# Narrow contractions unpadded, paired indexer units and earlier releases in a hybrid attention, mLSTM and MoE block

## The reference

```python
idx_score = einsum('bqh,bqhs->bqs', wib, relu(einsum('bqhd,bsd->bqhs', qib, ki)))   # 8 heads, d = 32
_, sel = lax.top_k(idx_score, 256)
logits = einsum('bqgrd,bqkgd->bqgrk', qb, ks) * scale                               # 8 heads, 2 key heads, d = 64
p = softmax(where(valid, logits, -inf)); out = einsum('bqgrk,bqkgd->bqgrd', p, vs)
```

```python
gu = xb @ w_gu[e] + b_gu[e]                   # 1024 x 2048 weights of each expert
act = glu * sigmoid(1.702 * glu) * (lin + 1)
y = act @ w_dn[e] + b_dn[e]                   # 1024 x 1024
```

## Time and profile before

| | us |
|---|---|
| median of three runs (2430.87 to 2431.50) | 2431.18 |
| the profiled execution | 2432.87 |
| its span, first to last instruction | 2431.1 |
| PE busy | 2223.4 (91%) |
| PE weight loads busy | 1799.6 (74%) |
| DVE busy | 1814.3 (75%) |
| ACT busy | 1374.4 (57%) |
| POOL busy | 527.8 (22%) |

### The profile page before, as it was taken

The page is one execution under the profiler, slowest core; times in us unless marked ns, Lnnn a source line. Parts: engine busy times, 40 slices in busy tenths (PEclk is TensorE's granted clock), DMA queues, the critical chain, the costliest instruction groups (busy, mean ns, idle before and its releaser), DMA issues.

```text
span 2431.1 us, 41797 instructions
## 1 busy us (share of the span) xinstructions
PE 2223.4 (91%) x15519; PEld 1799.6 (74%) x15519; DVE 1814.3 (75%) x2070; ACT 1374.4 (57%) x1547; POOL 527.8 (22%) x458
## 2 busy tenths in 40 slices
PE   6879999859979769999999999999999999999994
PEld 5667888748967557777777777777778778777773
DVE  3679999935442478778778778778877877877885
ACT  4451223756652346666666666666666657667664
POOL 1006786770020011111111111111101102102120
PEclk9989999869989879999999999999999999999997
DMA  5011211020012258798898898888989889889897
GB/s 142 13 35 35 53 51 45 31 83 1 1 51 104 101 211 311 278 332 299 295 332 289 304 323 306 308 316 301 315 303 318 316 294 325 315 281 333 314 323 273
DMA packets 253534, 526.47 MB, mean 217 GB/s; under 512 B 32984, under 2 KB 59736, under 8 KB 253116
## 3 DMA queue, kind: packets, MB, share of 16 engines
q1 hardware_dynamic: 240204, 483.27, 55.6%
q0 software_dynamic: 13264, 42.34, 6.7%
HBM read 490.96 MB, written 35.91 MB: 217 GB/s over the span
## 4 chain that ended last, share of the span: by engine, by line
PE 66%; DMA 10%; DVE 6%; ACT 5%; issue 5%; SPq 5%; POOL 4%; ACTq 0%; DVEq 0%; POOLq 0%
PE ps L1749 12%; PE ps L1751 11%; PE ps L1750 11%; DMA e_raw<-in_w_gate_up_dram 9%; PE ps L1428 6%; PE ps L1430 6%; PE ps L1429 6%; PE ps L1756 5%; PE ps L1629 2%; SPq L726 2%; PE ps L1619 1%; PE ps L1761 1%; DVE e_wlo L2256 1%; ACT e_whi L1311 1%; SPq L728 1%
## 5 line engine op out<-in xcount | busy, mean ns | idle before, releaser
L2256 DVE TENSOR_TENSOR e_wlo<-e_raw,e_whi 128x2048 fp32r<-128x2048 f32 x410 | 927.2, 2286 | 120.9 <-ACT e_whi L1311 118.1
L1311 ACT ACTIVATE e_whi<-e_raw 128x2048 fp32r<-128x2048 f32 x411 | 784.0, 1916 | 377.2 <-PE ps L1751 200.1
L1749 PE MATMUL ps<-e_whi,xh 128*128 128x512 f32 x1088 | 436.0, 401 | 6.4 <-DVE e_wlo L2256 6.2
L1750 PE MATMUL ps<-e_whi,xl 128*128 128x512 f32 x1088 | 424.5, 390 | 0.0
L1751 PE MATMUL ps<-e_wlo,xh 128*128 128x512 f32 x1088 | 424.2, 390 | 0.0
L937 POOL DMA_INDIRECT x_d<-ym,scur x34 | 71.8, 2110 | 926.2 <-ACT ym L1344 905.6
L1749 PEld LDWEIGHTS ps<-e_whi,xh 128*128 128x128 f32 x1088 | 204.2, 188 | 64.9 <-issue 23.9
L1749 PE MATMUL ps<-e_whi,ath 128*128 128x512 f32 x544 | 222.4, 409 | 22.3 <-DVE atl L2284 20.8
L1751 PEld LDWEIGHTS ps<-e_wlo,xh 128*128 128x128 f32 x1088 | 204.3, 188 | 44.1
L1750 PEld LDWEIGHTS ps<-e_whi,xl 128*128 128x128 f32 x1088 | 204.4, 188 | 38.8
L1751 PE MATMUL ps<-e_wlo,ath 128*128 128x512 f32 x544 | 214.0, 393 | 0.0
(11 more groups left out here) (358 smaller groups left out, 3562.5 us busy)
## 6 DMA issues: line engine op xcount, KB each, us to landing
e_raw<-in_w_gate_up_dram SPq DMA_DIRECT2D x275, 1024.0 KB, 6.3
e_raw<-in_w_down_dram SPq DMA_DIRECT2D x136, 1024.0 KB, 7.8
w_raw<-in_w_in_dram SPq DMA_DIRECT2D x20, 512.0 KB, 3.8
xt<-in_x_dram SPq DMA_DIRECT2D x8, 512.0 KB, 6.2
wo_raw<-in_w_out_dram SPq DMA_DIRECT2D x8, 512.0 KB, 6.7
xr<-in_x_dram SPq DMA_DIRECT2D x8, 512.0 KB, 4.3
x_d<-x SPq DMA_DIRECT2D x8, 512.0 KB, 2.6
h_d<-h SPq DMA_DIRECT2D x8, 512.0 KB, 2.9
```

The source lines that it names most:

```text
L1311: nc.scalar.activation(e_whi[:, m % HRING, :], e_raw[:, m % RING, :], ACT.Copy).then_inc(s.e_hi, 1)
L1749: nc.tensor.matmul(dst, a_hi, slot_hi, start=False, stop=False, skip_group_check=True)
L1750: nc.tensor.matmul(dst, a_lo, slot_hi, start=False, stop=False, skip_group_check=True)
L2256: nc.vector.tensor_tensor(e_wlo[:, m % HRING, :], e_raw[:, m % RING, :], e_whi[:, m % HRING, :].bitcast(F32), ALU.subtract).then_inc(s.e_l ...
```

## The change

1. **Indexer.** `iq_hi` and `iq_lo` keep the queries as they come, 128 rows by two groups of 128 columns. A head is a block of 32 rows of it, and the matmul takes these rows of queries and of keys alone. One copy on ACT and one subtraction on DVE make a query tile. PE issues two units at a time, each of the three terms for the one and then for the other, on different rows of the array. The units have four homes in PSUM (`unit_out`) in place of two. The five gate steps on ACT follow units 3, 6, 9, 12 and 15. POOL's zeroing of `iq_hi` and `iq_lo` is gone, and so is the wait for it.
2. **Attention.** `q_hi` and `q_lo` are kept the same way, four groups of 128 columns; a head is 64 rows. POOL's zeroing is gone. ACT's `k_hi` and first `q_hi` stand ahead of turn c = 8 of the mLSTM loop, and PE's `scores(0)` and `scores(1)` in turn c = 9, ahead of the last transposes of `m_hn`. PE's order is transposes(u), scores(u + 2), values(u - 1). The buffers that move for this put `wo_raw` elsewhere.
3. **Experts.** A piece whose slot was last used by an "S" or an "X" unit is loaded when DVE has made its low part (`e_lo`), no longer when PE has finished it. For slots last used by an "L" unit nothing changes.

```diff
-        iq_hi = at("iq_hi", Q0, [P, 2, IH, P], F32R)
+        iq_hi = at("iq_hi", Q0, [P, 2, 2, P], F32R)
...
-        q_hi = at("q_hi", M0, [P, 2, HEADS, P], F32R)
+        q_hi = at("q_hi", X0, [P, 2, 4, P], F32R)
...
+        def unit_out(u):
+
+            return ps[:, u % 4, :] if u < 2 * IH else pair(2 * ((u + 2) % 4))
...
             def load(u, m, e):
 
-                sp.wait_ge(s.p_pc, u.nth(PIECES, m + 1))
+                before = u.kind if m >= RING else {"L": "S", "S": "L", "X": "X"}[u.kind]
+                if before == "L":
+                    sp.wait_ge(s.p_pc, u.nth(PIECES, m + 1))
+                else:
+                    sp.wait_ge(s.e_lo, u.nth(PIECES, m + 1))
...
-                if f == 1:
-                    gp.wait_ge(s.p_ht, NT)
-                    nc.gpsimd.memset(iq_hi[:].bitcast(F32), 0.0)
-                    nc.gpsimd.memset(iq_lo[:].bitcast(F32), 0.0).then_inc(s.g_zero, 1)
...
-            gp.wait_ge(s.p_in, NT)
-            nc.gpsimd.memset(q_hi[:].bitcast(F32), 0.0)
-            nc.gpsimd.memset(q_lo[:].bitcast(F32), 0.0).then_inc(s.g_zero, 1)
...
-                        for g in range(4):
-                            rows = slice(ID * g, ID * g + ID)
-                            nc.scalar.activation(iq_hi[rows, i % 2, g::4, :], iqt[rows, :, i * P:(i + 1) * P], ACT.Copy).then_inc(s.a_iqhi, 1)
+                        nc.scalar.activation(iq_hi[:, i % 2, :, :], iqt[:, :, i * P:(i + 1) * P], ACT.Copy).then_inc(s.a_iqhi, 1)
...
-                        if u >= 22 and (u - 22) % 4 == 0 and (u - 22) // 4 < 5:
-                            gate_step((u - 22) // 4)
+                        if u in (3, 6, 9, 12, 15):
+                            gate_step(u // 3 - 1)
...
+                if c == NT:
+                    act.wait_ge(s.g_rq, 15)
+                    act.wait_ge(st_mo[0], 32)
+                    act.wait_ge(st_mo[1], 32)
+                    nc.scalar.activation(k_hi[:], kt[:], ACT.Copy).then_inc(s.a_qkhi, 1)
+                    q_hi_of(0)
...
-                if f == 5:
-                    pe.wait_ge(s.a_gate, 2)
+                if f in (4, 5):
+                    pe.wait_ge(s.a_relu, 6 * IH - 7 + f)
...
-            for u in range(6 * IH):
+            for u in range(0, 6 * IH, 2):
...
-                if u >= 2:
-                    pe.wait_ge(s.a_relu, u - 1)
+                if u == 2 * IH:
+                    pe.wait_ge(s.a_iwt, 1)
+                    pe.wait_ge(s.a_gate, 2)
+                elif u >= 4:
+                    pe.wait_ge(s.a_relu, u - 2)
...
-                    m = product(pair(2 * (u % 2))[:, a:b], iq_hi[:, i % 2, h, :], iq_lo[:, i % 2, h, :], ik_hi[:, a:b], ik_lo[:, a:b],
-                                True, True)
-                m.then_inc(s.p_is, 1)
+                    for n, (q_, k_) in enumerate(((iq_hi, ik_hi), (iq_hi, ik_lo), (iq_lo, ik_hi))):
+                        for e in range(2):
+                            rows = slice(ID * ((h + e) % 4), ID * ((h + e) % 4) + ID)
+                            m = nc.tensor.matmul(unit_out(u + e)[:, a:b], q_[rows, i % 2, (h + e) // 4, :], k_[rows, a:b],
+                                                 start=(n == 0), stop=(n == 2))
...
+                rows = slice(HD * (h // 4), HD * (h // 4) + HD)
+                    m = product(pair(2 * (u % 2))[:, a:b], q_hi[rows, i % 2, h % 4, :], q_lo[rows, i % 2, h % 4, :],
+                                k_hi[rows, a:b], k_lo[rows, a:b], True, True)
...
+                if c == NT + 1:
+                    pe.wait_ge(s.a_nd, NT)
+                    scores(0)
+                    scores(1)
...
                     transposes(u)
+                if u + 2 < NT * HEADS:
+                    scores(u + 2)
                 if u >= 1:
                     values(u - 1)
-                if u + 2 < NT * HEADS:
-                    scores(u + 2)
```

More of the change, by code:

```diff
@@ L706, in load, with loads @@
                     sp.dma_start(dn_piece(e_raw, slot), src).then_inc(s.ld_g[slot], 16)
-            def loads(u, here, following):
+            def loads(u, here, after, following):
                 for m in range(3, PIECES):
@@ L733, in _ @@
                 en = sp.value_load(be_d[bass.ds(j + ROW_X + 1, 1), 0:1], min_val=0, max_val=E - 1)
-                loads(Unit(j, 1, 2 * LARGE, "X"), ex, en)
+                loads(Unit(j, 1, 2 * LARGE, "X"), ex, "X", en)
             last = Unit(nl, 1, 2 * LARGE, "X")
             sp.wait_ge(s.st_yo, 16 * LARGE + 16)
-            for done, value in ((s.e_lo, last.nth(PIECES, 2)), (s.e_hi, last.nth(PIECES, 3)),
+            for done, value in ((s.e_lo, last.nth(PIECES, RING + 2)), (s.e_hi, last.nth(PIECES, 3)),
                                 (s.p_pc, last.nth(PIECES, RING)), (s.st_y, last.nth(16, 16))):
@@ L1224, in _ @@
             act.wait_ge(s.g_mix, NT)
-            act.wait_ge(s.g_rq, 15)
-            nc.scalar.activation(k_hi[:], kt[:], ACT.Copy).then_inc(s.a_qkhi, 1)
-            def q_hi_of(i):
-                if i == 0:
-                    act.wait_ge(s.g_zero, 4)
-                if i >= 2:
-                    act.wait_ge(s.p_s, HEADS * (i - 1))
-                for g in range(KVH):
-                    rows = slice(HD * g, HD * g + HD)
-                    nc.scalar.activation(q_hi[rows, i % 2, 4 * g:4 * g + 4, :], qt[rows, :, i * P:(i + 1) * P], ACT.Copy).then_inc(s.a_qkhi, 1)
-            q_hi_of(0)
             exp(0)
@@ L1598, in _ @@
                     m_weights(c + 1)
-            def scores(u):
-                i, h = u // HEADS, u % HEADS
-                w = P * (i + 1)
-                if u >= 2:
-                    pe.wait_ge(s.v_msk, u - 1)
-                if h == 0:
-                    pe.wait_ge(s.v_qklo, 2 * (i + 1) + 1)
-                for a in range(0, w, 512):
-                    b = min(a + 512, w)
-                    m = product(pair(2 * (u % 2))[:, a:b], q_hi[:, i % 2, h, :], q_lo[:, i % 2, h, :], k_hi[:, a:b], k_lo[:, a:b],
-                                True, True)
-                m.then_inc(s.p_s, 1)
             def transposes(u):
@@ L2011, in q_lo_of @@
             def q_lo_of(i):
-                for g in range(KVH):
-                    rows = slice(HD * g, HD * g + HD)
-                    dve.wait_ge(s.a_qkhi, 2 * i + g + 2)
-                    nc.vector.tensor_tensor(q_lo[rows, i % 2, 4 * g:4 * g + 4, :], qt[rows, :, i * P:(i + 1) * P],
-                                            q_hi[rows, i % 2, 4 * g:4 * g + 4, :].bitcast(F32), ALU.subtract).then_inc(s.v_qklo, 1)
+                dve.wait_ge(s.a_qkhi, i + 2)
+                nc.vector.tensor_tensor(q_lo[:, i % 2, :, :], qt[:, :, i * P:(i + 1) * P],
+                                        q_hi[:, i % 2, :, :].bitcast(F32), ALU.subtract).then_inc(s.v_qklo, 1)
             q_lo_of(0)
@@ L2201, in _ @@
             assert d.n == DEST_STEPS, d.n
+            dve.sem_inc(s.e_lo, RING)
+            dve.wait_ge(s.e_lo, RING)
             hot = Steps(dve, s.v_hot)
```

62 lines of the change are left out of this document (36 added, 26 removed).

## The result

The changed kernel is slower, by about 1%. Its median of ten executions is 2462.2 us (2440.43 to 2488.21), against 2431.42 us (2430.87 to 2433.78) for ten of the kernel before on the same chip, 31 us more. The ratio, which leaves the longest three executions out, is 1.0112 with a 95% interval of 1.0089 to 1.0135. The prediction was 2407.6 us. The ten times stand in three groups, near 2440, 2462 and 2487 us, with a mean granted clock of PE (the profile gives it as a share of full speed) of 0.932, about 0.921 and 0.910 to 0.915. The kernel before spreads over 3 us.

What follows compares the result with a forecast made beforehand. PE was taken to set the pace in most stages, DVE in the indexer, a short chain ahead of attention. Terms -14.5 - 7.1 + 14 - 16 = -23.6 us from the median of 2431.18 gave about 2407.6 us, range 2387 to 2424.

Steps and rivals of the forecast that it cites:

- the clock in attention: Attention: case of PE's clock staying low there, counted among the slower outcomes; chance 0.06.
- The sign that the prediction named: Sign that the forecast is wrong: a PE clock of 0.50 beyond the second query tile.
- Indexer: Indexer, query tiles 4 to 7: DVE no longer waits for relus, -14.5 us (bounds -8 and -18).
- The pairs of the indexer: Indexer, rival: paired units don't overlap on PE, 0 to 3 us; with clock 0.50 some 30 us lost, chance 0.04.
- Start of attention: Ahead of attention: the first exponential can start where `k_hi` did, -7.1 us (bounds -5 and -7.1).
- Attention itself: Attention units on PE: changes between 64 and 128 rows cost +14 us (bounds +22 and -3).
- Experts: Experts: earlier slot loads shorten PE's waits for `atl` (12 us) and `e_wlo` (4 us), -16 us (bounds -26 and -2).
- as the rival said: Experts, rival: the DMA stays the limit, -2 in place of -16, 2421.6 us; chance 0.13.
- The remark that the work can move: Experts: the DMA idles after the "S" unit, waiting for slots, so loading can move there; part of the -16 us.

Runs made afterwards that it cites:

- 64 rows from tile 2 on: Changed kernel with zero-padded keys, so scores use 128 rows, in query tiles 0 and 1 only; from tile 2 on 64 rows: 2387.95 us, 0.9815 to the kernel before.
- full rows: Changed kernel with keys kept twice, each copy zero outside its own key head, so attention scores use all 128 rows: 2373.02 us, 0.9758 to the kernel before.
- the old order: Changed kernel with PE's attention order put back to transposes(u), values(u-1), scores(u+2): 2436.34 us, 1.0049 to the kernel before.
- the pairs on one half: Changed kernel with attention heads scored in pairs, both heads of one key head on the same 64 rows: 2477.75 us, 1.0166 to the kernel before.
- the indexer's run in turn: Changed kernel with attention scores on 128 rows by padded keys, and the indexer pair's two units issued one after the other: 2377.04 us.

## Why the prediction was wrong

**The step that failed** is the clock in attention. The sum took the rise 18 us into attention from the kernel before and put a later one at nothing; a clock that stays low there was given 0.06. That case came true, and its size can be worked out from the rows: with the clock at 0.50 to the end, the 145 us from 558 us on the earlier trace rows would take up to twice as long, some 130 us more by the author's estimate, 2538 us in place of 2408. Measured are 2488 us, for a clock that rises 185 us later than before. The sign that the prediction named, a clock of 0.50 beyond the second query tile, is what the trace shows. The chance was weighed wrongly. What spoke for a low one, that the transposes and value matmuls, most of the records, are unchanged, counts records. By time the scores are a third of a unit of tile 7 (1.47 of 4.06 us), and the runs show that whether the other half of the array works beside them decides over 83 us. Up to the rise before, PE was busy with matmuls on the whole array for 16.92 of 18 us; what that would be worth without "whole array" was not asked.

The loss by the clock is 99 us in the profiled execution and 74 at the medians (2462.2 against 2387.95). The 99 us: the second row of the table of spans is 508.4 us, and 409.0 in the run that keeps the clock up with 64 rows from tile 2 on. The rest of the stages agrees within 2 us.

**Indexer**, -14.5 us: right, and a little more. The four large tiles took 37.2 us (105.23 to 142.40) where 38.2 were worked out. Tile 4 starts 2.6 us earlier (105.23, not 107.85). 2.1 of that lie ahead of the indexer (its first step on DVE starts at 87.43, not 89.53), so tiles 2 and 3, to which a loss of 0 to 2 us was given, gained 0.5. PE's wait for the gate rows ends 18.5 us earlier, just beyond the bound of -18. 15.7 of them reach the end of the mLSTM group. Its turn with the two copies on ACT is 1.3 us longer (11.27 us between two `m_hn` of ACT, 10.01 before), where the prediction had them hidden; that the copies are the whole cause isn't shown, and the other 1.6 us aren't traced.

**The pairs of the indexer** do run at once: start 0.01 us apart, six matmuls of 512 columns in the time of three. The rival said that the lack of it would cost 30 us with the clock at 0.50; it cost 16.5. The clock was at 0.50 there (88 to 142 us), as that rival feared, and with the pairs it did no harm: PE needs six distances of 0.42 us, 2.5, for a pair of 1024 keys, DVE 2.8. The sum had said that the overlap hardly matters, at 0.227 us for a matmul; at the clock of this trace twelve in turn take 5.1 us. So the indexer's term came out by an overlap that it didn't count on, which is luck. In the trace the second of a pair starts 6 ns behind the first, and the next two 0.42 us later (131.57, 131.99 us).

**Start of attention**, -7.1 us: exact. From the last `mixt` to the first exponential it took 8.43 us (531.27 to 539.70) and takes 1.30 (515.56 to 516.86). The forecast of 518 for it was missed by 1.

**Attention itself**, +14 us: the price of the changes is right, if one leaves the clock out. A unit of tile 7 costs 0.34 us more at clock 1.00 (4.05 to 4.39), where 0.26 was taken and 0.34 was the value by the earlier trace rows. Over the tiles 2 to 7 it is 14.9 us against full rows. The full rows themselves are 5.6 us faster than before from the first exponential to the first `ym` (394.4 against 400.0). The clock that rises 5.8 us sooner after the first exponential (12.8 against 18.6) makes up 2.9 us of it, an estimate at half the clock; the rest isn't shown. So the net is +9 us. The trace shows late starts at the changes to and from 64 rows too: the differences of the unit shown above are 0.10 us for transposes, 0.12 for scores and 0.11 for values.

**Experts**, -16 us: the sign was right, the size was half. Measured -31.0. The stop for `atl` in the "S" units was to fall by 0.75 us each; it fell by 0.35 (16.8 to 11.2 us in sixteen). The DMA is still full there (share 1.04), as the rival said, and a split still waits 0.79 us for its weights. What was missed lies elsewhere: the "L" units fell from 51.1 to 50.0 us each, 16 us in the fifteen between the first and the last `ym` (in one of them, 1156.60 to 1207.50 us before and 1239.30 to 1289.30 now, PE stood still for 0.32 us and now for nothing; where the rest of its 0.9 us lies isn't shown); the two "X" units, of which the prediction didn't speak, fell from 84.3 to 75.2. The remark that the work can move into the idle time after an "S" unit fits: the DMA's share there rose from 0.29 to 0.92.

Put together with the measured sizes and a clock that rises: -15.7 - 7.1 + 9 - 31 = -45, 2387 us. The run with 64 rows from tile 2 on took 2387.95. That is no test of the sum, since the +9 comes from this run; it shows that nothing is left over.

**What stays open.** The three groups of times fit a clock that rises at different moments: the shorter executions have a higher mean clock, 0.921 and 0.932. Both profiles of this kernel show the latest rise, 742.9 and 741.9. The profile with the old order, of the group at 0.932, has it at 634.9, which is what an earlier rise looks like, though in a kernel with one edit more. What picks the group isn't known. It is open as well why the clock fell back in the pairs on one half but not with 64 rows from tile 2 on: the two differ in the pause of PE and in how long the scores on one half last without a break, and neither was changed alone. How idle rows and changes share the delay is known only from the table above, one profile for each row.

## What to carry to other kernels

Before taking zero rows out of a matmul, ask what PE's clock is at that point and what is to raise it: padding cost PE no time here (4.00 us for a unit on full rows, 4.39 on 64), and with rows that stood idle the clock was 0.50 for 226 us of the stage. If narrow contractions are wanted, put another one beside them on the other rows (here the clock rose after 41.3 us), or use them only behind a stretch of full-array work that has brought the clock up (here it stayed at 1.00 for 167 us). The second rests on one run, in which PE hardly paused; look at the granted clock afterwards. A case whose price is five times the expected gain (130 us by the estimate above, against 23.6) deserves a look at what it depends on, not only a small chance.

## What the runs showed of the hardware

- With PE busy for 225.5 of 227 us on scores of 64 rows, the granted clock was 0.50 throughout; with two heads on both halves of the array it rose to 1.00 after 41 us, with full rows after 13. In the indexer it was 0.50 for 72 us with PE busy for 71.86, on 32 rows.
- What the clock was before matters: the same 64-row scores ran at 1.00 for 167 us in one kernel, after full-row scores had raised the clock, and at 0.50 for 227 us in the other.
- Matmuls on other rows overtake: two products of three matmuls, issued one after the other, start 0.01 us apart on different 32 rows (130.49 us in the indexer's run in turn) and on different 64 rows (548.29 us); with six matmuls ahead, on different 64 rows, the second product starts 0.59 us late.
- The two changes between 64 and 128 rows in a unit of tile 7 cost 0.34 us at clock 1.00: 4.39 us in the changed kernel, 4.05 before.
- The engines worked side by side: of the 2486.4 us of the changed kernel's profiled execution PE was busy for 2315.3, DVE for 1805.5, ACT for 1365.1 and POOL for 555.9. SP issued the 411 loads of `e_raw`, 1024 KB each. Where one needs what another makes it waits: PE for `atl` of DVE 18 times, 14.0 us.
